# Two small logits per head and token: a padded 128-column projection tile against 64 narrow matmuls on untouched FP32 data

## The reference, cut to what matters

```
p = x @ w_in                                   # 1024 x 6160
b_logit = rest[..., GDN_VAL:GDN_VAL + 8]       # 8 columns of p
a_logit = rest[..., GDN_VAL + 8:]              # 8 columns of p
beta = sigmoid(b_logit)
g = -exp(a_log) * softplus(a_logit + dt_bias)
gc = cumsum(g) within chunks of 64 tokens
```

## Time and profile before

| | |
|---|---|
| median of three executions | 3716.8 us |
| the profiled execution, whole | 3722.02 us |
| its span | 3720.3 us |
| TensorE busy | 3483.1 us, 94% of the span |
| VectorE busy | 1708.8 us, 46% |
| ScalarE busy | 1102.5 us, 30% |
| GpSimd busy | 446.4 us, 12% |
| TensorE's mean granted clock | 0.965 of full speed |

### The profile page before, as it was taken

The page is one execution under the profiler, slowest core; times in us unless marked ns, Lnnn a source line. Parts: engine busy times, 40 slices in busy tenths (PEclk is TensorE's granted clock), DMA queues, the critical chain, the costliest instruction groups (busy, mean ns, idle before and its releaser), DMA issues.

```text
span 3720.3 us, 45988 instructions
## 1 busy us (share of the span) xinstructions
PE 3483.1 (94%) x19022; PEld 2504.7 (67%) x19022; DVE 1708.8 (46%) x3340; ACT 1102.5 (30%) x2244; POOL 446.4 (12%) x746
## 2 busy tenths in 40 slices
PE   8999989999998989999879899999999999999998
PEld 6776875776677577577453344478854488888886
DVE  3533443344353435435416889766632232333424
ACT  4432442243243324124212111256631121111112
POOL 0210120011021423012510011100000000000000
PEclk9999999999999989999978999999999999999999
DMA  2200110100001011011110012200030011111111
GB/s 94 75 30 17 40 36 1 41 29 24 29 29 41 12 37 35 23 40 29 49 71 35 23 62 72 71 1 1 1 142 34 23 46 46 57 46 46 57 46 45
DMA packets 36523, 151.96 MB, mean 41 GB/s; under 512 B 4983, under 2 KB 9657, under 8 KB 28890
## 3 DMA queue, kind: packets, MB, share of 16 engines
q1 hardware_dynamic: 36314, 149.03, 11.6%
HBM read 133.28 MB, written 15.73 MB: 40 GB/s over the span
## 4 chain that ended last, share of the span: by engine, by line
PE 83%; DVE 6%; ACT 4%; POOL 3%; issue 2%; DMA 1%; SPq 0%; POOLq 0%; DVEq 0%; ACTq 0%
PE pp L563 7%; PE pp L565 7%; PE pp L564 7%; PE pp L1224 6%; PE pp L1226 6%; PE pp L1225 6%; PE pp L1059 6%; PE pp L733 5%; PE pp L1206 3%; PE pp L1190 2%; PE pp L884 2%; PE pp L1154 2%; PE pp L1138 2%; PE pp L1049 2%; PE pp L931 1%
## 5 line engine op out<-in xcount | busy, mean ns | idle before, releaser
L563 PE MATMUL pp<-gx_hi,pw_hi 128*128 128x512 f32 x1168 | 485.8, 416 | 29.0 <-DVE pw_lo L1814 28.1
L565 PE MATMUL pp<-gx_hi,pw_lo 128*128 128x512 f32 x1168 | 466.7, 400 | 0.0
L564 PE MATMUL pp<-gx_lo,pw_hi 128*128 128x512 f32 x1168 | 466.2, 399 | 0.0
L563 PEld LDWEIGHTS pp<-gx_hi,pw_hi 128*128 128x128 f32 x1168 | 226.3, 194 | 77.7 <-DVE pw_lo L1814 30.9
L1224 PE MATMUL pp<-x_hi,wt_hi 128*128 128x512 f32 x704 | 274.6, 390 | 1.1 <-DVE x_lo L2361 1.1
L1226 PE MATMUL pp<-x_hi,wt_lo 128*128 128x512 f32 x704 | 274.1, 389 | 0.0
L1225 PE MATMUL pp<-x_lo,wt_hi 128*128 128x512 f32 x704 | 274.1, 389 | 0.0
L565 PEld LDWEIGHTS pp<-gx_hi,pw_lo 128*128 128x128 f32 x1168 | 225.5, 193 | 49.9
L564 PEld LDWEIGHTS pp<-gx_lo,pw_hi 128*128 128x128 f32 x1168 | 226.6, 194 | 43.7
L733 PE MATMUL pp<-xT,arena 128*128 128x512 f32 x512 | 233.8, 594 | 6.3 <-DVE arena L1990 6.3
L1814 DVE TENSOR_TENSOR pw_lo<-arena,pw_hi 128x1024 fp32r<-128x1024 f32 x73 | 89.6, 1229 | 241.1 <-ACT pw_hi L1279 241.1
(11 more groups left out here) (399 smaller groups left out, 6533.9 us busy)
## 6 DMA issues: line engine op xcount, KB each, us to landing
arena<-in_tiles_dram SPq DMA_DIRECT2D x73, 512.0 KB, 3.6
arena<-in_units_dram SPq DMA_DIRECT2D x33, 1024.0 KB, 4.9
xT<-in_w_outs_dram SPq DMA_DIRECT2D x6, 2048.0 KB, 8.6
xT<-in_wall_dram SPq DMA_DIRECT2D x6, 2048.0 KB, 8.4
w<-in_wall_dram SPq DMA_DIRECT2D x4, 2048.0 KB, 8.3
gates_scratch<-arena SPq DMA_DIRECT2D x32, 256.0 KB, 2.4
arena<-gates_scratch SPq DMA_DIRECT2D x8, 1024.0 KB, 5.0
arena<-in_xT_dram SPq DMA_DIRECT2D x8, 512.0 KB, 8.4
```

The source lines that it names most:

```text
L563: mm(b[:, hs], wh[:, c], X[0][:, k, hs], k == 0, False)
L564: mm(b[:, hs], wh[:, c], X[1][:, k, hs], False, False)
L565: m = mm(b[:, hs], wl[:, c], X[0][:, k, hs], False, k == 7)
```

## The change: what it does

The padded tile is gone. `w_ba` is laid out as 8 slices of 16 columns, 64 KB, in a buffer of its own, `wba`. TensorE computes the logits straight in token-major form: for each of 8 blocks of 128 tokens it accumulates 8 plain FP32 matmuls with a 128x128 block of the unsplit input as the stationary operand and 16 columns of `wba` as the moving one. These 64 matmuls stand behind tile 4 and directly ahead of the wait for `gg`. ScalarE's and VectorE's splits of `w_ba`, the copy out of PSUM and the 8 transposes go. `rates` and `decays` of ScalarE and VectorE are now one function, in the same order as before. The load of `x` into `y` moves up from behind the load of tile 7 to behind that of tile 3, and waits for nothing but that tile's turn.

```diff
             def half(u, b, hf):
-                wh, wl = PW[u % 2] if u != "ba" else ba_W
+                wh, wl = PW[u % 2]
...
-            def decay_logits():
-                b = place_(R["v"], ("proj", "ba"), ("bac",))
-                for hf in range(2):
-                    run(half("ba", b, hf))
-
-            def turn_logits():
-                b = place_(Ring([7]), ("ba",), ("ga",))
-                pe.wait_ge(("bac",), ("ident",))
+            def decays():
+                ring = Ring([7])
+                b = place_(ring, ("ba",), ("ga",))
+                pe.wait_ge([("d", f"xT{hf}{i}") for hf in range(2) for i in range(4)], ("d", "w_ba"))
                 for n in range(8):
-                    m = tr(b[:, n * 16:(n + 1) * 16], baT[:, n * 128:(n + 1) * 128], ident[0:16, 0:16])
+                    for k in range(8):
+                        m = mm(b[:, n * 16:(n + 1) * 16], stage[n // 4][:, k, n % 4 * 128:n % 4 * 128 + 128],
+                               wba[:, k * 16:(k + 1) * 16], k == 0, k == 7)
                 m.then_inc(*did("ba"))
-
-            def decays():
-                b = place_(Ring([7]), ("gcs",), ("gtmp",))
+                b = place_(ring, ("gcs",), ("gtmp",))
                 pe.wait_ge(("gg",), ("U",), ("ones",))
...
-                    run(tiles(g, [3]))
-                    decay_logits()
-                    steps = tiles(g, [4])
-                    for _ in range(2):
-                        next(steps)
-                    turn_logits()
-                    run(steps)
+                    run(tiles(g, [3, 4]))
                     decays()
...
-                    ac.wait_ge(("d", "w_ba"))
-                    act(ba_W[0], ba_raw, ACT.Copy).then_inc(*did("ph", "ba"))
...
-                    dv.wait_ge(("ph", "ba"), ("d", "w_ba"))
-                    tt(ba_W[1], ba_raw, ba_W[0].bitcast(F32), ALU.subtract).then_inc(*did("pl", "ba"))
...
-            col(ba_raw, "w_ba")
+            col(wba[:, :], "w_ba")
...
-                    if u == 6:
-                        sp.wait_ge(("proj", "ba", 1), ("ba",))
+                    if u == 2:
                         move(y[:, :, :], I["x"].rearrange("(n p) d -> p n d", p=128), "y", "d", "y")
```

More of the change, by code:

```diff
@@ L200, in program @@
         small = sb("small", [128, 832])
+        wba = sb("wba", [128, 128])
         PP = [ctx.enter_context(nc.psum_tensor(f"pp{i}", [128, 1024], F32))[:, :] for i in range(4)]
@@ L222, in program @@
         tile_place[48], tile_place[49] = arena[:, 6144:7168], arena[:, 5120:6144]
-        y_flat = y.rearrange("p n d -> p (n d)")
-        ba_raw, baT = y_flat[:, 0:1024], y_flat[0:16, 3072:4096]
-        ba_W = [over(f"ba_{c}", 1024, F32R, "y", 1024 * (i + 1)) for i, c in enumerate(("hi", "lo"))]
         take = cutter(arena, AR - 1024)
@@ L557, in half @@
                         yield
-                    if u == "ba" or u < 48:
+                    if u < 48:
                         pe.wait_ge(("xl", hf, k))
@@ L1845, in tiles, with decays @@
                         values(g, i - 1)
-            def rates():
+            def decays():
                 b = at("ba")
@@ L2034, in dve_program @@
                     run(tiles(g, [3, 4]))
-                    rates()
                     decays()
@@ L2930, in arrays @@
         "gdn_nw": f["gdn_norm_w"][0].reshape(2, 128).T,
-        "w_ba": cols(np.pad(wi[:, 6144:6160], ((0, 0), (0, 112)))),
+        "w_ba": cols(wi[:, 6144:6160]),
         "gdn_a_log": f["gdn_a_log"][0],
```

## The result

The changed kernel took 3741.4 us as the median of four executions (3737.18 to 3741.95) against 3719.41 us for the four of the kernel before: ratio 1.0057, 95% interval 1.0039 to 1.0075. Five later executions of it (changed_again) had a median of 3738.07 us against 3719.96, ratio 1.0049 (1.0037 to 1.0062). It is slower, by 18 to 22 us of the medians. (The ratios in this document are those of the means.) The profiled execution took 3742.49 us, with a span of 3740.8 us, 20.5 us more than the span before.

The account below looks back on a forecast made before the run. TensorE, busy 94% of the span, was taken as the bound. With 11.7 us gone, 24.8 + 5.4 + 0.9 us put tile 5 18.9 us later; less 0.9 given back, 18 more: 3740 profiled, 3735 median, range 3731 to 3739.

Parts of the forecast that it names:

- the run at half clock: TensorE behind tile 4: 128 narrow passes, 25 at full clock, then 103 at 0.215 us each, 24.8 us in all.
- the open wait: Behind the logits TensorE stands still for g, formerly hidden beside tile 4: 5.4 us, bounds 4.9 and 6.7.
- the median, 3716.8, is 5.2 us lower, and I carry the difference over to the median: Sum made on the profiled execution, 3722.02 us, slowest of three; their median lies 5.2 us lower, so 3740 becomes 3735.
- give-back: Around tile 5: less idling than before, so the clock may stay up; 0.9 us given back, bounds 0 and 1.7.
- rival 2: The early load of x hinders tile 3's load, TensorE waits 3.6 us more: 3738.5 us, chance 5%.
- What goes: On TensorE's path: the padded tile, 11.0 us, and the 8 transposes in tile 4, 0.7 us; together 11.7 us.
- The cumulated sums: 4 passes on TensorE behind the wait for g: 0.86 us at half clock instead of 0.45, 0.4 us more.
- Rival 1: The narrow passes stay at 0.107 us, 13.7 us for the run: 3723 us, chance 8%.
- Rival 3: The narrow passes pack at 0.033 us each, 4.2 us for 128, so not slower: 3715 us, chance 3%.
- rival 4: rates has run by the time it is waited for, so the 5.4 us stall is absent: 3729 us, chance 3%.

Follow-up runs that it names:

- before_again: The kernel before, unchanged, executed and profiled once more: one execution, 3720.5 us.
- logits_ahead_of_tile4: The changed kernel with the 64 narrow matmuls ahead of tile 4 instead of behind it: 3736.8 us, ratio to before 1.0047.
- logits_spread_tile2: The changed kernel with its 64 narrow matmuls dealt out in tile 2, four behind each step of three dense ones: 3721.5 us, ratio to before 1.0000.
- logits_twice: The changed kernel with the 64 narrow matmuls made twice over, with the same results: 3765.0 us, ratio to before 1.0125.
- x_load_late: The changed kernel with the load of x put back behind the load of tile 7: 3740.8 us, ratio to before 1.0060.
- logits_spread: The changed kernel with its 64 narrow matmuls dealt out two behind each step of three dense ones in tiles 2 and 3: 3728.2 us, ratio 1.0031.

## Why the prediction was right or wrong

**The direction and the mechanism** were right, the run at half clock and the open wait both. The forecast was 18 us more; the first comparison gave 22.0, the second 18.1. The nine executions of the changed kernel that the two comparisons count have a median of 3738.1 us (3739.3 with the first profiled one, 3742.49, as the tenth), and the 63 of the kernel before that were timed along the way one of 3719.9, which makes 18.2 (19.4). That this comes so close to 18 is in part luck. Two terms, told below, came out 2.0 to 2.4 us too low together, and at the counterpart of L600 the two profiles of the changed kernel stand 18.6 to 21.2 us behind the two of the kernel before, 19.9 on average; what an execution does with its clock later on moves the whole by more than that.

**The absolute time** was not: 3735 against 3741.4, and the range ended at 3740. The step that failed is "the median, 3716.8, is 5.2 us lower, and I carry the difference over to the median". That was a median of three. The 63 executions run from 3711.3 to 3729.8, and their median is 3 us above those three's: 2.1 us should have been taken off the profiled execution, not 5.2. On 3719.9 the same sum gives 3738. This is not the whole miss. Against the base of its own comparison, 3719.41, the 6.4 us part into 2.6 of base and 4.0 of shift, 22.0 for 18, and either alone would have stayed within the range. Of the 4.0 the profile shows 3.2 at the counterpart of L600 (21.2 us later for 18): the narrow run 1.1 us longer and begun 1.2 us later, and a give-back of 0.9 that did not come. The range allowed "some us" for scatter, up to 3739 and stretched to 3740 for rival 2; that was too little above a base that was 3 us low, for executions from 3737.2 to 3742.0. The second comparison, at 3738.1, lies within it.

**What goes**, 11.7 us: right as far as it can be seen; tile 4 takes 11.0 us without the transposes (71.63 to 82.65). The two splits that went can't be seen: the first sums of squares start at 50.51 and 50.95 us in the changed kernel's two profiles, at 50.99 and 51.14 in those of the kernel before.

**The run at half clock** was right in kind and 1.1 to 1.5 us short: 25.94 and 26.35 us for 24.8. The pace was right (0.21 us a pass). The fall came 1.7 and 1.2 us into the run, not 2.7. In the first profile the run also began 1.2 us late, at 84.35 for 83.2, because the fall in the first sums of squares lasted 10.2 us instead of 6.8. before_again has such a long fall too, so this belongs to the execution and not to the change.

**The open wait**, 5.4 us, was right to the row, with the first table load off the chain, and logits_ahead_of_tile4 shows it as a cost of its own. The cumulated sums took 0.84 us for 0.86.

**The give-back** of 0.9 us did not come. I had tile 5's slow start swallow 2.6 of 3.4 us of idle time, so that the clock would stay up later. The clock came back after 3.7 us of tile 5, not 5.3; 1.96 us of idle time were left, and the clock fell again behind it, for 3.4 us, as before the change.

**Rival 1**, passes at 0.107 us, is refuted in the changed kernel and true in logits_spread_tile2: the matmuls are the same, the clock is not. That answers the Trainium skill's rule as well ("TensorE: Matmul & The Clock Gate", "LDWEIGHTS (loading the stationary operand)"): 107 ns for 128 columns agrees with the trace at full clock (the changed kernel's 16 passes from 82.65 to 84.35 us, 0.106 each), and logits_twice's 0.214 us a pass contradicts it at half clock. The rows give the pace of a whole pass, load and matmul together. **Rival 2**, x in the way of tile 3, is refuted by x_load_late. **Rival 3**, passes that pack, and **rival 4**, a wait that isn't there, by the rows above.

A rival that I did not name is that plain FP32, and not the few moving columns, brings the clock down. The kernel before has plain FP32 matmuls of 512 columns too: L1059, 256 matmuls in 512 records, half of them on the tiles of the row below. In the 100 us of the second row they are 215 of the 239 records, and the clock is 1.00:

```profile
L1059 PE MATMUL pp<-w,xT x256: 592/592/697, 2166.5 to 2399.0; 128*128 128x512 f32 x128
2200.00:2300.00 100.00, 100.00 (x239) 42.27 (x238) 96.12 (x137) 19.96 (x37) 18.09 (x16) 1.00 0.23 82
```

So the type alone does not do it, though other work stands between these too. How many columns a pass must move for the clock to hold was not measured.

## What to carry to other kernels

Count a small matmul by its weight loads and ask what the array does meanwhile: 64 matmuls of 16 columns were no cheaper at full clock (14.5 us, 128 passes at the pace of logits_spread_tile2) than the 48 of 512 columns that they replaced (11.0), and as a block of their own they ran at half clock. In this kernel narrow matmuls belonged among dense ones, in a stretch where the clock was already up, with other work between them and whoever waits for what they lead to; even there they gained nothing over the padded tile (ratio 1.0000). Where weight columns are padding, put something into them: high and low part side by side saved a third of the passes. And before a forecast is put on a median, look at how far the executions scatter.

## What the runs showed of the hardware that was not expected

What the clock does depends on where it stands. The same mix of dense and narrow matmuls, one step after the other, ran at 1.00 for 17.6 us in tile 2 of logits_spread, where it began at 1.00, and at 0.50 for 34.3 us in tile 3, where it began at 0.50. In between lay only 3.7 us of sums of squares. Both stretches are of one profile; that it is so in every execution is not shown. A denser share of narrow passes still held 1.00 for 24.4 us in logits_spread_tile2.

The spread of this kernel's executions, 18 us over 63 of them, goes with the time at half clock: in the 59 whose granted clock is on record a thousandth less clock goes with 3.3 us more span, and a thousandth of 3720 us is 3.7. In five profiles that make the same later work (before, before_again, the changed kernel, changed_again, x_load_late) the spans reach from 3718.8 to 3740.8 us, and the remainders only from 3586.1 to 3590.3.
